# A hybrid mLSTM and state-space layer on one core: twelve gate tiles as three rounded products

## The reference

```
h = modulate(rmsnorm(x, norm_mix), shift1, scale1)
q, k, v, o, gates, u, ga, gb = jnp.split(h @ w_in, IN_SPLITS, axis=-1)
# (A) mLSTM on q, k, v, o, gates;  (B) S5 state-space branch on u:
bu = einsum('gpc,btgc->btgp', b_bar, u);  xs = associative_scan(a_bar, bu)
y  = real(einsum('gcp,btgp->btgc', c_c, xs))        # forward and backward
h_b = gelu(z) * sigmoid(z @ w_glu + b_glu),  z = yf + flip(yb) + s5_d * u
merged = sigmoid(ga) * (h_a @ w_pA) + sigmoid(gb) * (h_b @ w_pB)
out = merged @ w_out
# then a residual, and an expert-choice MoE of 16 experts
```

## Time and profile before

| | us |
|---|---|
| median of 3 runs | 1642.82 (1641.87 to 1645.7) |
| the profiled execution, its own time | 1642.62 |
| its span | 1640.7 |
| block U | 44.3 to 86.5 |
| state-space block | 86.5 to 277.2 |
| granted clock over the span, mean | 0.98 |
| busy over the span: PE, DVE, ACT, POOL | 1552.6, 687.7, 371.1, 135.2 |

### The profile page before, as it was taken

One profiled execution on the slowest core, in us unless ns is written; L12 is line 12 of the kernel. 1 busy time (PEld: TensorE's weight loads), 2 busy tenths in 40 slices (PEclk: granted clock), 3 DMA queues, 4 the chain that ended last, 5 costly groups with the idle time before them and its releaser, 6 DMA issues. The chain is left out here.

```text
span 1640.7 us, 35064 instructions
## 1 busy us (share of the span) xinstructions
PE 1552.6 (95%) x15908; PEld 1107.5 (67%) x15908; DVE 687.7 (42%) x1418; ACT 371.1 (23%) x716; POOL 135.2 (8%) x192
## 2 busy tenths in 40 slices
PE   5999999999999999899959999999999999999994
PEld 2456665889899897899945766667777544444552
DVE  7878994423424253688461112222222122222214
ACT  5254433332433334555330000000000000000001
POOL 0000000000000000242030011111110011110001
PEclk9999999999999999999979999999999999999997
DMA  9355455021211111535249999999999999999985
GB/s 389 129 152 161 140 186 215 9 104 52 78 52 29 57 45 68 218 111 218 77 145 403 424 415 415 415 415 414 416 420 419 416 415 416 414 416 415 425 367 173
DMA packets 58154, 420.39 MB, mean 256 GB/s; under 512 B 11460, under 2 KB 18756, under 8 KB 28308
## 3 DMA queue, kind: packets, MB, share of 16 engines
q1 hardware_dynamic: 51172, 391.71, 59.2%
q0 software_dynamic: 6544, 25.37, 5.1%
q10 hardware_dynamic: 288, 1.05, 0.2%
HBM read 391.55 MB, written 24.42 MB: 254 GB/s over the span
## 5 line engine op out<-in xcount | busy, mean ns | idle before, releaser
L2032 PE MATMUL bank<-place,hT 128*32 128x384 f32 x3120 | 262.0, 490 | 11.3 <-issue 9.1
L2032 PE MATMUL bank<-ring_tail,hT 128*32 128x384 f32 x3024 | 252.0, 486 | 2.6 <-DMA ring_tail<-w_e_dram 2.4
L2032 PEld LDWEIGHTS bank<-place,hT 128*32 128x32 f32 x3120 | 127.2, 111 | 137.3 <-issue 70.3
L2032 PEld LDWEIGHTS bank<-ring_tail,hT 128*32 128x32 f32 x3024 | 125.9, 110 | 121.7 <-issue 53.7
L2133 DVE TENSOR_TENSOR xT<-sq,bank 128x384 f32<-128x384 f32 x48 | 23.7, 550 | 373.4 <-PE bank L2032 348.3
L2082 ACT ACTIVATE sq<-bank 128x384 f32<-128x384 f32 x48 | 20.1, 491 | 701.3 <-PE bank L2032 701.3
L2104 DVE SCALAR_TENSOR_TENSOR hT<-bank,gvr,xT 32x256 f32<-32x256 f32 (+1 forms) x192 | 92.1, 480 | 206.4 <-PE bank L2053 203.9
L2053 PE MATMUL bank<-place,xT 128*32 128x256 f32 x2304 | 131.1, 383 | 4.0 <-DMA place<-w_e_dram 4.0
L2053 PE MATMUL bank<-ring_tail,xT 128*32 128x256 f32 x2304 | 130.1, 380 | 1.2 <-DMA ring_tail<-w_e_dram 1.2
L2053 PEld LDWEIGHTS bank<-place,xT 128*32 128x32 f32 x2304 | 99.7, 111 | 33.5 <-DMA place<-w_e_dram 6.0
L2053 PEld LDWEIGHTS bank<-ring_tail,xT 128*32 128x32 f32 x2304 | 99.4, 111 | 29.8 <-issue 1.9
(11 more groups left out here) (422 smaller groups left out, 2280.4 us busy)
## 6 DMA issues: line engine op xcount, KB each, us to landing
place<-w_e_dram SPq DMA_DIRECT2D x97, 1536.0 KB
ring_tail<-w_e_dram SPq DMA_DIRECT2D x95, 1536.0 KB
place<-w_ada_dram SPq DMA_DIRECT2D x12, 2048.0 KB, 9.8
place<-w_qk_dram SPq DMA_DIRECT2D x4, 2048.0 KB, 8.3
place<-w_vo_dram SPq DMA_DIRECT2D x4, 2048.0 KB, 8.3
xT<-w_gate_dram POOLq DMA_DIRECT2D x7, 1024.0 KB, 5.9
place<-w_pAB_dram SPq DMA_DIRECT2D x4, 1536.0 KB, 6.4
hT<-gates_dram SPq DMA_DIRECT2D x4, 1280.0 KB, 5.9
```

Of the source, the lines that this page charges most:

```text
L2032: mm = pe.matmul(PS[bank + j][TJ * g:TJ * g + TJ, 0:FC], x[:, e % 2, j, 2 * c + k, :], w[:, k, FC * g:FC * g + FC], start=(c == 0 and k == 0),
```

## The change

- In the state-space block, gate tiles 1 to 12 become three rounded products of 320 columns per half and step: 48 products a tile. Tile 0 stays fp32.
- ACT rounds hT to h_high at the start of block U (before: at the start of the mLSTM block), and rounds the weights of tile u + 1 (round_gate, 128 x 1024) in act_gate of tile u, ahead of its sigmoid.
- DVE makes h_low in quarter 0 (before: in the mLSTM block), and the low part of each tile's weights (split_gate, 128 x 1024) at three places in the quarter: after coefficients_in, before the scans, and after the last step on the states.
- The copies of the states to Xp (place_states) and of bb to bbz (place_inner) go from DVE to ACT. The negation of CA[:, 1] on DVE goes; ACT's copies to CAo and bbz carry a scale of -1 in its place.
- ACT's four exponentials for rows_ready go from after the first transposed coefficients to the end of block U.
- Gate weights come one tile at a time (512 KB); there is one staging buffer; several buffers lie elsewhere (Kt, kd and negM in spare, the new ones in place of s5bc and others). In the mLSTM block one DVE copy of negM is added.

```diff
             for k in range(KD):
-                w = gw[:, u // 2 % 2, k, (u % 2) * P:(u % 2 + 1) * P]
-                pe.matmul(PS[banks[0]][:, :], w, hT[:, k, 0:LAT], start=(k == 0), stop=(k == 7))
-                mm = pe.matmul(PS[banks[1]][:, 0:CTX], w, hT[:, k, LAT:TOK], start=(k == 0), stop=(k == 7))
+                for x in range(2):
+                    t = slice(x * TH, (x + 1) * TH)
+                    if u == 0:
+                        mm = pe.matmul(PS[banks[x]][:, 0:TH], gw[0][:, k, :], hT[:, k, t], start=(k == 0), stop=(k == 7))
+                        continue
+                    for i, (w, h) in enumerate(((gw_high, h_high), (gw_high, h_low), (gw_low, h_high))):
+                        mm = pe.matmul(PS[banks[x]][:, 0:TH], w[u % 2][:, k, :], h[:, k, t], start=(k == 0 and i == 0),
+                                       stop=(k == 7 and i == 2))
             mm.then_inc(sem("gate_done"), 1)
...
+        def round_gate(act, u):
+
+            if u < NU_S5:
+                act.wait_ge(sem(f"gate_w{u % 2}"), 16 * (u // 2 + 1))
+                if u >= 2:
+                    act.wait_ge(sem("gate_done"), u - 1)
+                act.activation(gw_high[u % 2][:], gw[u % 2][:], ACT.Copy).then_inc(sem("split_high"), 1)
+
+        def split_gate(dve, u):
+
+            if u < NU_S5:
+                dve.wait_ge(sem("split_high"), KD + u)
+                dve.tensor_tensor(gw_low[u % 2][:], gw[u % 2][:], gw_high[u % 2][:].bitcast(F32),
+                                  ALU.subtract).then_inc(sem("split_low"), 1)
...
+            round_gate(act, u + 1)
             act.wait_ge(sem("gate_done"), u + 1)
...
                 for m in range(4):
                     out_u(m)
+                act.wait_ge(sem("m_ready"), 1)
+                for d in range(2):
+                    act.activation(R[:, 2 + d, 0:LAT], Mx[:, d, 0:LAT], ACT.Exp, bias=gpar[:, 4 + d:5 + d], scale=-1.0)
+                    ins = act.activation(R[:, 4 + d, :], cum[:, d, :], ACT.Exp, scale=-1.0)
+                ins.then_inc(sem("rows_ready"), 1)
...
+                def place_states(q):
+                    act.wait_ge(sem("xfin_ready"), q + 1)
...
+                    for r in range(2):
+                        act.activation(Xp[F, r, :, 0:JL], V[F, r, :, 0:JL], ACT.Copy)
+                        act.activation(Xp[F, r, :, JL:J], V[F, r, :, JL + 1:NS_ - 1], ACT.Copy)
+                        act.activation(Xp[B, r, :, 0:JL], V[B, r, :, 0:JL][:, :, ::-1], ACT.Copy)
+                        ins = act.activation(Xp[B, r, :, JL:J], V[B, r, :, JL + 1:NS_ - 1][:, :, ::-1], ACT.Copy)
+                    ins.then_inc(sem("xp_copied"), 1)
...
                         turned_coefficients(q + 1, 1)
+                    place_states(q)
                     gate()
...
+                        dve.wait_ge(sem("gate_done"), 1)
+                        for k in range(KD):
+                            dve.wait_ge(sem("split_high"), k + 1)
+                            dve.tensor_tensor(h_low[:, k, :], hT[:, k, :], h_high[:, k, :].bitcast(F32),
+                                              ALU.subtract).then_inc(sem("split_low"), 1)
+                        split_gate(dve, 1)
...
                         coefficients_in(dve, v, q + 1)
+                    split_gate(dve, 3 * q + 2)
...
                     v(dve.tensor_tensor(V[:, 1], tz[:, 2], tz[:, 3], ALU.subtract))
+                    split_gate(dve, 3 * q + 3)
...
+                    if q + 1 < NQ:
+                        split_gate(dve, 3 * q + 4)
                     dve_ada(dve, 4 + 2 * q, 7)
```

More of the change, by code:

```diff
@@ L589, in coefficients_out @@
                 p(eng.tensor_tensor(tb_, pi, br, ALU.mult))
-                p(eng.tensor_tensor(CA[:, 1], ta, tb_, ALU.add))
-                eng.tensor_scalar(CA[:, 1], CA[:, 1], -1.0, 1.0, ALU.mult, ALU.mult).then_inc(sem("ca_ready"), 1)
+                eng.tensor_tensor(CA[:, 1], ta, tb_, ALU.add).then_inc(sem("ca_ready"), 1)
                 eng.wait_ge(sem("ca_ready"), q + 1)
@@ L619, in _ @@
             def _(pool):
-                pool.wait_ge(sem("xpos_out"), 16)
-                for half in range(2):
-                    load_gate(pool, half)
+                load_gate(pool, 0)
             @block.tensor
@@ L649, in _ @@
                 a = chain(act, "act")
+                act.wait_ge(sem("xpos_out"), 16)
+                for k in range(KD):
+                    act.activation(h_high[:, k, :], hT[:, k, :], ACT.Copy).then_inc(sem("split_high"), 1)
                 act.wait_ge(sem("gate_abs"), 1)
@@ L899, in additions, with place_inner @@
                                        ACT.Copy).then_inc(sem("v_copied"), 1)
+                def place_inner(q):
+                    g = slice(QG * q, QG * q + QG)
+                    if q == 0:
+                        act.wait_ge(sem("bbz_ready"), 1)
+                    for d, own in enumerate((F, B)):
+                        for r in range(2):
+                            ins = act.activation(bbz[own, d, r], bb[own, r, g, :], ACT.Copy, scale=1.0 - 2.0 * r)
+                    ins.then_inc(sem("bbz_ready"), 1)
+                def place_states(q):
+                    act.wait_ge(sem("xfin_ready"), q + 1)
+                    if q:
+                        act.wait_ge(sem("s5_y_done"), 2 * q)
+                    else:
+                        act.wait_ge(sem("u_out1"), 32)
+                    for r in range(2):
+                        act.activation(Xp[F, r, :, 0:JL], V[F, r, :, 0:JL], ACT.Copy)
[3 more added lines that the diff above has]
+                    ins.then_inc(sem("xp_copied"), 1)
+                place_inner(0)
                 turned_coefficients(0, 0)
                 turned_coefficients(0, 1)
-                act.wait_ge(sem("m_ready"), 1)
-                for d in range(2):
-                    act.activation(R[:, 2 + d, 0:LAT], negM[:, d, 0:LAT], ACT.Exp, bias=gpar[:, 4 + d:5 + d])
-                    ins = act.activation(R[:, 4 + d, :], cum[:, d, :], ACT.Exp, scale=-1.0)
-                ins.then_inc(sem("rows_ready"), 1)
                 gate()
@@ L951, in _ @@
                 cx = slice(JL + 1, NS_)
-                v(dve.memset(bbz[:], 0.0))
+                dve.memset(bbz[:], 0.0).then_inc(sem("bbz_ready"), 1)
                 for q in range(NQ):
                     g = slice(QG * q, QG * q + QG)
-                    if q:
-                        dve.wait_ge(sem("s5_lag_done"), q)
-                    for d, own in enumerate((F, B)):
-                        for r in range(2):
-                            ins = dve.tensor_copy(bbz[own, d, r], bb[own, r, g, :])
-                    ins.then_inc(sem("bbz_ready"), 1)
                     v(dve.memset(Et[:, 0, :, 0:1], 1.0))
@@ L1364, in _ @@
                 act.wait_ge(sem("gate_out1"), 16 * 6)
-                for k in range(KD):
-                    act.activation(h_high[:, k, :], hT[:, k, :], ACT.Copy).then_inc(sem("split_high"), 1)
                 round_weights(0)
@@ L1463, in _ @@
                                     ).then_inc(sem("z_in"), 1)
-                for k in range(KD):
-                    dve.wait_ge(sem("split_high"), k + 1)
-                    dve.tensor_tensor(h_low[:, k, :], hT[:, k, :], h_high[:, k, :].bitcast(F32),
-                                      ALU.subtract).then_inc(sem("split_low"), 1)
                 split_weights(0)
@@ L1482, in _ @@
                              for x in (og[0:H, 1], hacc[0:H]))
-                v(dve.tensor_copy(high.bitcast(F32R), negM[:]))
-                v(dve.tensor_tensor(rest, negM[:], high, ALU.subtract))
+                v(dve.tensor_copy(rest, negM))
+                v(dve.tensor_copy(high.bitcast(F32R), rest))
+                v(dve.tensor_tensor(rest, rest, high, ALU.subtract))
                 v(dve.tensor_copy(mid.bitcast(F32R), rest))
```

88 lines of the change are left out of this document (48 added, 40 removed).

## The result

| | us | runs |
|---|---|---|
| before | 1642.59 | 4 (1641.87 to 1645.7) |
| changed | 1662.14 | 4 (1660.7 to 1665.13) |

The ratio is 1.0121, with a 95% interval of 1.0105 to 1.0136: the change costs 19.5 us. The forecast was 1651.5, within 1640 to 1660. The sign was right, the forecast size (8.9) was less than half of the measured one, and the time lies 2 us outside the range.

The account below looks back on a forecast made before the run. PE was taken as the bound, DVE nearly one. Entry with quarter 0 +3.0, quarters 1 and 2 +3.7, PE reaching lags(3) after DVE +0.2, quarter 3 -2.0, clock +4.0: +8.9, giving 1651.5 us, range 1640 to 1660.

Parts of the forecast that it names:

- What PE saves: Gate tiles on PE: rounded products at 0.147 us each save 1.6 us a tile, 4.8 a quarter, 19 for twelve.
- What DVE's chain becomes: DVE, full quarter: work 42.1 us plus a new 4.1 wait for ACT makes 46.2 against 44.36, 1.85 slower.
- The entry: Start of the state-space block: exponentials before the border open it at 90.4, +3.9; DVE's transposed rows are there at 104.6.
- Quarter 0 on DVE: DVE's steps from 104.6 to the end of coefficients_out at 150.0, against lags at 147.02 before: +3.0, entry included.
- PE's clock: Half clock after PE's gaps at the entry and in quarter 2, +2.0 each: +4.0.
- The fall in quarter 1 is absorbed: PE's clock fall in quarter 1 delays nothing directly, since PE waits for DVE again.
- Quarter 3: From lags to the block's last product: 39.1 us, against 41.05 before, -2.0.
- Loads beside the projection's are late: Rival: gate loads take 11.2 us, +5.6 in quarter 0 and +5.6 in quarter 3, 1662; chance 0.07.
- PE stays the bound: Rival: DVE's chain with waits takes under 39.6 us a quarter, tiles give their 19 us, 1628.4; chance 0.11.
- DVE's rows are one chain: Argument against the rival that PE stays the bound: DVE's profile rows in the state-space block form one chain.

Follow-up runs that it names:

- shorter tiles: Kernel before, with gate tiles 1 to 12 summing 6 of their 8 steps (gates not the reference's): 1625.08 us, ratio 0.9895.
- last version: The version with four edits of order, plus tile 3q + 2 rounded right behind the Kt copies and place_inner(0) behind the first CT copies: 1631.26 us, ratio 0.9942.
- light neighbour: Changed kernel, with projection loads on SP's queue, from the second in the state-space block on, bringing 256 of 4096 columns: 1656.95 us, ratio 1.0081.
- rounding first: Changed kernel, with ACT's rounding of tile 3q + 4 put ahead of the copies of the states: 1657.2 us, ratio 1.0088.
- exponentials early: Changed kernel, with ACT's four exponentials ahead of out_u(3), the last copy of block U: 1656.94 us, ratio 1.0089.
- four edits of order: Changed kernel; earlier: rounding of 3q + 4 (before state copies), exponentials (before out_u(3)), gate load (before store), subtraction for 3q + 2 (before coefficients_in): 1648.96 us, ratio 1.0045.

## Why the prediction came out short

The mechanism that was forecast is there: a wait of 4.5 us a quarter behind the copies of the states, which makes DVE's cycle longer than before. What failed are the sizes of two terms of the sum, quarter 0 and PE's clock, and quarter 3 with them.

- **"What PE saves"** held: 0.146 us a product. **"What DVE's chain becomes"** held nearly: a cycle of 46.8 for 46.2. The copies took 3.41 for 3.0, the wait 4.53 for 4.1. Its parts are confirmed one by one: 42.36 for 42.4 with the work of before (shorter tiles), 42.15 for 42.1 with the new work and no wait (last version).
- **"The entry"**: the block opened at 91.3, 0.9 later than the 90.4 (0.7 of that was there at the start of block U), and DVE had the transposed rows at 107.43, for 104.6 + 2.0 with the clock. Right within 0.8.
- **"Quarter 0 on DVE"** is the first mis-sized term. Against its own steps: rows +0.8; the wait for Kt +1.6, since the small products and lags ran at half clock; the rounding of tile 2 +0.9, which I had costed at nothing; the load of tile 3 +3.6; the copies +0.4. That is 7.3 of the 7.2 by which lags(1) is late. The load was issued 3.8 later than the 122.7 (120.7 and the clock): 2.0 since PE's tile 1 ended later, 1.6 since ACT's sigmoid stood behind its copies of CA and a rounding. It landed after 8.4 us, where I took 5.6 and had 11.2 as a bound. I had bounded its price by rows and left its issue time to one value.
- **"PE's clock"** is the second. I counted falls at two places for +4.0. Keeping PE at work at the entry gives back 4.9, and in the quarters 4.0: 8.9 in separate runs (they were not run together, so that the sum is an estimate). That is 4.9 of the 10.6 us by which the sum was short; the entry's share of it lies in part in quarter 0 above and is not to be added to it. Three things failed in it. The entry's gap was followed by a second fall, behind gate tile 0, which I had costed at nothing. "The fall in quarter 1 is absorbed" was wrong: DVE had its coefficients at 204.61 + 1.36 = 205.97, PE came to lags at 207.99, and with the gap filled lags came at DVE's pace. And I had no fall before outputs(3), behind a gap of 4.06 us. The rule of the Trainium skill that I drew on ("TensorE: Matmul & The Clock Gate", Part 1: The HAM clock gate), that the throttle is what the clock returns to in idleness, bore out at the restarts: gaps of 5.5, 7.0, 5.3 and 4.1 us each ended at half clock. What did not bear out is my reading of the rows: I set 7.04 against 1.77 us as if the length of a gap decided. The same trace of the kernel before has a gap of 1.64 us, at 282.88, behind which its clock is 0.50 for four us.
- **"Quarter 3"**: 39.1 predicted, 43.5 measured. Step by step: the subtraction for tile 12 is done at 20.7 for 19.6 us after lags (+1.1; its load took 6.5 for 5.6), the eight copies take 3.4 for 3.0 (+0.4), and from outputs to the end it is 11.4 for 8.5 (+2.9), for outputs begin at half clock behind the gap of 4.06. So the gain that I had booked went mostly to the clock.
- **Rivals.** "Loads beside the projection's are late" (0.07, 1662; its own terms add up to 1651.5 + 11.2 = 1662.7) gives the measured number, but by luck: the loads came at 8.4 us, not 11.2, and the clock made the rest. "PE stays the bound", 1628.4, did not happen. That the last version reaches 1631.3, near its number, does not bear out its mechanism either, a DVE chain under 39.6 us: the chain takes 42.15. My argument against it (DVE's rows are one chain) held in every order that was run. What the order of the queues withheld is the part between 42.15 and 44.36; in the last version the block's last product ends 9.9 us earlier than before, and 2.8 us of its gain lie behind the block, where no run says what of.
- The range failed because my bounds were taken as independent. The bounds for the copies and the load held, the waits for Kt and for tile 2 had none, and in this trace the terms come together: a later load makes a longer gap on PE, and behind the gap the clock is low.

## What to carry over

Before moving work off an engine that is nearly the bound, list for each new semaphore what stands ahead of its producer on that producer's in-order queue: here 4.5 us a quarter went to a rounding standing behind eight copies, though its input had long been there. Place a preparing step (round, split, load) where its input arrives, not where its consumer stands; and when one such wait is gone, look for the next one behind it before costing the gain. A gap on PE costs its own length and then the clock after it, which here was about twice what I had counted; unread products in the gaps gave back 4.9 us at the entry and 4.0 in the quarters. And when a run comes out at the expected total, check the step that was to bring it: with the light neighbour the load did land earlier, but much of the trace's gain had other causes.

## What the hardware showed that I had not expected

- After a restart the clock can fall a second time while PE is busy: 0.50 and 0.67 from 108 to 116 us in the changed kernel, 0.52 and 0.62 in the kernel before with the exponentials moved, with PE busy for all of it, on products of 80 and 128 columns. In the kernel before the same products ran at 1.00. With the gap at the border cut from 5.49 to 0.34 us they ran at 0.82 and 0.75. And with the full gap of 5.49 they ran at 1.00 in the traces of the two kernels with the rounding first and with the light neighbour. So neither the gap nor the products decide it alone, and what does stays open.
- The length of a gap does not decide either, except at the long end. In the traces up to 300 us, the clock over the four us behind a gap of 5.3 to 7.0 us was 0.50 to 0.58 every time. Behind one of 2.2 to 4.6 it was 0.50 to 0.63, but 1.00 behind one of 2.58 (exponentials early) and one of 2.87 (rounding first). Shorter ones go both ways: 1.59 and 1.77 at the opening brought 0.58 from 104 to 108 in the early-exponentials kernel, 1.59 and 1.78 brought nothing in the version with four edits of order. In the kernel before, 1.77 at the opening brought nothing, but behind this gap of 1.64 the clock is 0.50 over the next four us:

```profile
282.88 2.05 PE L1121 MATMUL bank<-Pm,qk 128*128 128x512 f32 x2 [1.64 <-DVE Pm L1462]
```

- A gate load of 512 KB took 8.4 us in quarter 0 of the changed kernel beside a load of 2 MB, and 4.8 when that neighbour was cut to a sixteenth. The median of its twelve loads in the block is 4.7.
